# The expert stage takes its first 128 tokens ahead of the rest, and projects its routing heads in another order

## What is computed

```python
h2 = _modulate(x, norm2_g, shift2, scale2)            # RMS norm, gain, shift
qp = (h2 @ w_pq).reshape(b, s, PEER_HEADS, 2, PEER_HALF)      # 8 heads, 2 halves of 128
sc = einsum("bshpd,hpnd->bshpn", qp, sub_keys)        # 128 keys per half
s1, i1 = top_k(sc[..., 0, :], 16); s2, i2 = top_k(sc[..., 1, :], 16)
cand = s1[..., :, None] + s2[..., None, :]            # 256 candidates
top_s, top_c = top_k(cand, 16)
expert = i1[top_c // 16] * 128 + i2[top_c % 16]; gate = softmax(top_s)
# per token, 8 heads x 16 experts:
a = h2 . peer_u[expert]; w = gate * gelu(a); y = sum(w * peer_v[expert])
x = x + gate2 * y
```

## Time and profile before

| | us |
|---|---|
| median of 3 runs (3081.39 to 3085.98) | 3084.47 |
| the profiled execution, whole | 3083.38 |
| its span in the profile | 3081.6 |
| expert stage, from its first load to the end | 1707.9 to 3081.6 |

### The profile page before, as it was taken

One profiled execution on the slowest core, in us unless ns is written; L12 is line 12 of the kernel. 1 busy time (PEld: TensorE's weight loads), 2 busy tenths in 40 slices (PEclk: granted clock), 3 DMA queues, 4 the chain that ended last, 5 costly groups with the idle time before them and its releaser, 6 DMA issues. The chain is left out here.

```text
span 3081.6 us, 36160 instructions
## 1 busy us (share of the span) xinstructions
PE 2484.2 (81%) x12224; PEld 1695.7 (55%) x12224; DVE 2154.5 (70%) x3952; ACT 1006.6 (33%) x2029; POOL 1190.1 (39%) x971
## 2 busy tenths in 40 slices
PE   6998969999999798678899798766676667766665
PEld 5998969999999694244566443322222222222222
DVE  6346856777777885576334477777777878778776
ACT  2223135666666322233233222222222221222221
POOL 1444456666666430111003133443434344434442
PEclk8999989999999898787999999988889888888888
DMA  3233621221111162000301499999999999999998
GB/s 103 79 102 98 191 82 56 62 61 54 54 56 54 48 191 68 22 8 1 82 1 48 185 382 418 406 421 406 421 421 418 394 421 421 416 394 421 421 421 337
DMA packets 269756, 666.40 MB, mean 216 GB/s; under 512 B 13989, under 2 KB 201546, under 8 KB 203834
## 3 DMA queue, kind: packets, MB, share of 16 engines
q0 software_dynamic: 73728, 536.90, 42.2%
q1 hardware_dynamic: 194906, 127.75, 14.1%
q10 hardware_dynamic: 992, 0.13, 0.0%
HBM read 662.64 MB, written 2.10 MB: 216 GB/s over the span
## 5 line engine op out<-in xcount | busy, mean ns | idle before, releaser
L2106 PE MATMUL peer_py<-peer_uv,peer_diag 128*128 128x512 f32 x1536 | 841.6, 695 | 362.1 <-ACT peer_diag L2026 361.7
L1794 POOL DMA_INDIRECT peer_uv<-k_peer_uv,peer_idx x512 | 501.0, 978 | 772.6 <-PE peer_py L2106 727.9
L1906 DVE SCALAR_TENSOR_TENSOR peer_spare<-peer_uv,peer_hp 128x1024 bf16<-128x1024 f32 x512 | 622.4, 1217 | 236.5 <-DMA peer_uv<-k_peer_uv,peer_idx 236.3
L2106 PEld LDWEIGHTS peer_py<-peer_uv,peer_diag 128*128 128x128 f32 x1536 | 320.4, 221 | 844.4 <-issue 837.1
L2018 ACT ACTIVATE peer_ga<-peer_a 128x2 f32<-128x2 f32 x256 | 52.0, 203 | 843.8 <-DVE peer_spare L1906 843.8
L890 POOL TENSOR_TENSOR hgrn_wl<-p2n_w,hgrn_wh 128x1024 fp32r<-128x1024 f32 x64 | 152.5, 2393 | 231.7 <-ACT hgrn_wh L927 231.7
L1023 PE MATMUL hgrn_pp<-p2n_hh,hgrn_wh 128*128 128x264 f32 x1024 | 219.0, 295 | 17.5 <-POOL p2n_hl L340 16.7
L1023 PE MATMUL hgrn_pp<-p2n_hh,hgrn_wl 128*128 128x264 f32 x1024 | 209.6, 286 | 0.0
L1023 PE MATMUL hgrn_pp<-p2n_hl,hgrn_wh 128*128 128x264 f32 x1024 | 209.6, 286 | 0.0
L2026 ACT ACTIVATE peer_diag<-keep_ident,peer_wt 128x128 f32<-128x128 f32 x384 | 140.1, 396 | 112.1 <-DVE peer_wt L1915 111.5
L1023 PEld LDWEIGHTS hgrn_pp<-p2n_hh,hgrn_wh 128*128 128x128 f32 x1024 | 160.1, 191 | 20.7 <-issue 14.6
(11 more groups left out here) (396 smaller groups left out, 4867.2 us busy)
## 6 DMA issues: line engine op xcount, KB each, us to landing
p2n_w<-in_hgrn_w_in SPq DMA_DIRECT2D x64, 512.0 KB, 4.0
p1n_w<-in_pool_w_in SPq DMA_DIRECT2D x32, 512.0 KB, 4.0
pool_out_aw<-in_w_ada SPq DMA_DIRECT2D x16, 768.0 KB, 4.7
hgrn_out_aw<-in_w_ada SPq DMA_DIRECT2D x16, 768.0 KB, 4.9
pool_out_w<-in_pool_w_out SPq DMA_DIRECT2D x8, 1024.0 KB, 7.5
p_w<-in_w_pq SPq DMA_DIRECT2D x8, 1024.0 KB, 16.0
peer_uv<-k_peer_uv,peer_idx POOLq DMA_INDIRECT x512, 12.4
fox_wq<-in_w_in SPq DMA_DIRECT2D x12, 512.0 KB, 6.4
```

Source lines behind the costliest of these rows:

```text
L1794: pool.indirect_dma_start(out=uv[:, n % DEPTH].rearrange("p w d -> p (w d)"), out_offset=None, in_=io["k_peer_uv"], in_offset=bass.Indirec ...
L1906: dve.scalar_tensor_tensor(out=spare[:, n % 2, :], in0=uv[:, n % DEPTH, 0, :], scalar=1.0, in1=hp[:, t % 2, :], op0=ALU.mult, op1=ALU.mult ...
L2106: last = pe.matmul(py[:, h * 512:(h + 1) * 512], diag[:, products(n) % DIAGS, :], uv[:, n % DEPTH, 1, h * 512:(h + 1) * 512], start=n % (P ...
```

## The change

Three things change in `peer_phase` and the `Norm` that it uses.

1. The norm works in two spans: tokens 0 to 127 (reciprocal, eight products, eight shifts), then tokens 128 to 511. ScalarE adds the second span's shifts after it has copied the first scores.
2. Heads 0 and 1 are projected for the first 128 tokens alone, both halves in one bank with one copy (`FIRST`), and the other 384 tokens of these heads (`REST`, four pieces) later: three ahead of unit 0, the fourth in unit 0 at k = 1. Units 0 and 1 are scored right after their `FIRST` piece.
3. Head s+2 (before: s+3) is projected within unit s, for s = 0 to 5: at k = 4 and 7 in unit 0, at k = 1 and 4 in the others. ScalarE takes its halves at pairs 3 and 4 in unit 0 and at pairs 1 and 3 in the others. The scores of unit s+2 follow at k = 9 (unit 0) or k = 7, and ScalarE copies them at pair 4, that is after k = 8 and 9. VectorE routes unit s+2 in six slots, two pieces for each k from 10 to 15, for s = 0 to 5. From unit 6 on all is as before.

The weights of heads 2 and 3 are loaded when head 0, and head 1, have been projected in full. `part` is renamed `running`.

```diff
     def dve(self, dve):
         dve.wait_ge(self.rooted, 1)
-        dve.reciprocal(self.rs[:, :], self.rs[:, :]).then_inc(self.own, 1)
-        dve.wait_ge(self.own, 1)
-        for c in range(KC):
-            dve.scalar_tensor_tensor(out=self.out[:, c, :], in0=self.x[:, c, 0:self.tokens], scalar=self.gain(c),
-                                     in1=self.rs[:, :], op0=ALU.mult, op1=ALU.mult).then_inc(self.scaled, 1)
+        for i, (a, b) in enumerate(self.spans):
+            dve.reciprocal(self.rs[:, a:b], self.rs[:, a:b]).then_inc(self.own, 1)
+            dve.wait_ge(self.own, i + 1)
+            for c in range(KC):
+                dve.scalar_tensor_tensor(out=self.out[:, c, a:b], in0=self.x[:, c, a:b], scalar=self.gain(c),
+                                         in1=self.rs[:, a:b], op0=ALU.mult, op1=ALU.mult).then_inc(self.scaled, 1)
...
+        FIRST, REST, WHOLE = (0, P), (P, SEQ), (0, SEQ)
+        parts = [(0, None, FIRST), (1, None, FIRST)] + [(n, j, REST) for n in range(2) for j in range(2)] + \
+            [(n, j, WHOLE) for n in range(2, PH) for j in range(2)]
+        part_at = {e: i for i, e in enumerate(parts)}
...
             for n in range(2, PH):
-                sp.wait_ge(projected, 2 * (n - 1))
+                sp.wait_ge(projected, part_at[n - 2, 1, REST if n < 4 else WHOLE] + 1)
                 load(sp, n, n % 2)
...
-                if s == 0:
-                    return [p for p in (2 * (k - 9), 2 * (k - 9) + 1) if 0 <= p < 11]
+                if s + AHEAD < PH:
+                    return [p for p in (2 * (k - 10), 2 * (k - 10) + 1) if 0 <= p < 11]
                 return [k - 3] if 3 <= k < 14 else []
...
             norm.act(act)
-            take_q(0, 0)
-            take_q(0, 1)
+            take_q(0, None, FIRST)
             take_c(0)
+            norm.shifts(act, 1)
             act.wait_ge(x_turned, 1)
             act.activation(g2[:, :], py[:, :], ACT.Copy).then_inc(x_taken, 1)
-            take_q(1, 0)
+            take_q(1, None, FIRST)
+            take_c(1)
             take_x(0)
             exps(0)
-            take_q(1, 1)
-            take_c(1)
+            take_q(0, 0, REST)
+            take_q(0, 1, REST)
+            take_q(1, 0, REST)
             exps(1)
...
-                    if s == 0 and at in (0, 1):
-                        take_q(2, at)
-                    if s == 0 and at == 2:
-                        take_c(2)
-                    if s == 0 and at in (4, 6):
-                        take_q(3, 0 if at == 4 else 1)
-                    if s and at in (3, 5) and s + 3 < PH:
-                        take_q(s + 3, 0 if at == 3 else 1)
+                    if s == 0 and at == 1:
+                        take_q(1, 1, REST)
+                    if s + 2 < PH and at == (1 if s else 3):
+                        take_q(s + 2, 0, WHOLE)
+                    if s + 2 < PH and at == (3 if s else 4):
+                        take_q(s + 2, 1, WHOLE)
+                    if s + 2 < PH and at == 4:
+                        take_c(s + 2)
                     if at == 6 and s + AHEAD < UNITS:
                         exps(s + AHEAD)
-                if s + 3 < UNITS:
+                if PH <= s + 3 < UNITS:
                     take_c(s + 3)
...
             norm.pe(pe)
-            project(0, 0)
-            project(0, 1)
+            project(0, None, FIRST)
             scores(0)
             turn_h(0)
...
-            project(1, 0)
+            project(1, None, FIRST)
+            scores(1)
             pe.wait_ge(x_taken, 1)
             turn_x(0)
-            project(1, 1)
-            scores(1)
-            project(2, 0)
+            project(0, 0, REST)
+            project(0, 1, REST)
+            project(1, 0, REST)
...
                     if s == 0 and k == 1:
-                        project(2, 1)
-                    if s == 0 and k == 4:
-                        scores(2)
-                    if s == 0 and k in (6, 9):
-                        project(3, 0 if k == 6 else 1)
-                    if s and k in (2, 6) and s + 3 < PH:
-                        project(s + 3, 0 if k == 2 else 1)
-                    if k == (12 if s else 13) and s + 3 < UNITS:
+                        project(1, 1, REST)
+                    if s + 2 < PH and k == (1 if s else 4):
+                        project(s + 2, 0, WHOLE)
+                    if s + 2 < PH and k == (4 if s else 7):
+                        project(s + 2, 1, WHOLE)
+                    if s + 2 < PH and k == (7 if s else 9):
+                        scores(s + 2)
+                    if k == 12 and PH <= s + 3 < UNITS:
                         scores(s + 3)
```

More of the change, by code:

```diff
@@ L319, in act, with shifts @@
                        bias=self.keep["eps"][:, 0:1], scale=1.0 / D).then_inc(self.rooted, 1)
+        self.shifts(act, 0)
+    def shifts(self, act, span):
+        a, b = self.spans[span]
         for c in range(KC):
-            act.wait_ge(self.scaled, c + 1)
+            act.wait_ge(self.scaled, span * KC + c + 1)
             if self.shift is not None:
-                act.activation(self.out[:, c, :], self.out[:, c, :], ACT.Identity, bias=self.shift(c))\
+                act.activation(self.out[:, c, a:b], self.out[:, c, a:b], ACT.Identity, bias=self.shift(c))\
                    .then_inc(self.ready, 1)
@@ L1938, in store @@
                 dve.wait_ge(x_taken, t + 2)
-                dve.tensor_tensor(rows[:, t % 2, :], py[:, :], part[:, :], ALU.add).then_inc(scaled, 1)
+                dve.tensor_tensor(rows[:, t % 2, :], py[:, :], running[:, :], ALU.add).then_inc(scaled, 1)
                 dve.wait_ge(scaled, 2 * t + 1)
```

50 lines of the change are left out of this document (30 added, 20 removed).

## The result

The changed kernel takes 3090.11 us (median of 20 runs, 3087.13 to 3094.78), the kernel before 3082.46 (20 runs beside them, 3078.91 to 3086.74). The ratio is 1.0024, with a 95% interval of 1.0018 to 1.0030: 7.6 us slower. 3093 had been forecast, within 3077 to 3103.

The account below looks back on a forecast made before the run. The expert stage was taken as bound by gathers, with DMA full at 418 GB/s. Terms -2.6 + 13.0 - 3.1 = +7.3, plus 2 for the clock, gave +9.3 on 3083.4, 3092.7, called 3093 us; range 3077 to 3103.

Parts of the forecast that it names:

- First gather: Start-up up to the first gather: it was to come 13.6 us earlier (11.5 to 15), at 1731.2.
- First product: TensorE's first product, after the start-up projections: at 1750.0 instead of 1764.28, 14.3 us earlier.
- Unit 0: TensorE is the path; two k's take 3.44 us, and head 2's projection waits 2.4 us for weights landing at 1764.5.
- Scores, route, second dot of unit 1: Head 2's scores at 1786.0, VectorE's 18.2 us behind them, second dot starting at 1804.2; only 2.6 us gained.
- Units 1 to 5: Projection, scores and routing in one unit: 44.6 us each, 223.0 for five, 13.0 us more than before.
- Lead given back: In unit 6 the gathers set the pace again and a lead of 3.1 us is given back.
- Clock: TensorE's lower clock at the start of one of five units (k = 0 and 1): +2 us, ends 0 and +10.6.
- rival D: TensorE's lower clock at the start of every unit: 3102 us in all; chance 0.12.
- A: The forecast itself: units 1 to 5 paced by loop product, `take_q`, scores and route, 3086 to 3100 us; chance 0.45.
- Rival B: The eight buffers absorb the waits, units stay at 42.0 us and the early start is kept: 3073.4 us; chance 0.15.
- Rival C: Same loop but 2 us shorter in each unit (42.6 us), about even: 3084 to 3086 us; chance 0.20.
- Rival E: Weights and clock leave the first gather only 9 us earlier, costing 2 to 4 us on A: 3096 us; chance 0.08.

Follow-up runs that it names:

- experiment 3: Changed kernel with one half head projected a unit ahead: 3085.46 us; with the other half and the scores early too: 3082.62 us.
- experiment 6: Eight redundant TensorE instructions (3.43 us) ahead of the first half of heads 4 to 7: changed kernel 3101.74 us, kernel before 3092.57 us.
- Experiment 4: Changed kernel with the old unit order, head 2 projected whole ahead of unit 0, remaining tokens of heads 0 and 1 in units 5 and 6: 3069.17 us.

## Why the prediction was right, and where it wasn't

All times of after are less 4.71.

- **First gather**: forecast 1731.2, measured 1730.5. Head 0 started at 1713.5 (1714 taken), and the weights were what it waited for. The 32 instructions took 5.90 (6.2 forecast).
- **First product**: forecast 1750.0, measured 1749.2.
- **Unit 0**: forecast a wait of 2.4 us for head 2's weights. There was none to be seen: the load issued at 1744.75 was in when TensorE came to it at 1769.07, at most 24.3 us later, which fits the 23.8 of the earlier trace rows. TensorE came 2.3 us later than forecast because the first two k's ran at the lower clock (6.57 us to 1760.47, 3.44 had been taken) after 3.17 us of idleness. So head 2's projection started at 1764.4, where 1764.5 had been forecast by way of a wait that wasn't seen. That this time came out is luck: the step that failed is "two k's are 3.44". Whether a TensorE 2.3 us earlier would have met the wait no run shows.
- **Scores, route, second dot of unit 1**: forecast 1786.0 and 1804.2, measured 1785.8 and 1803.7. The 18.2 us that VectorE has behind the scores were 18.0.
- **Units 1 to 5**: forecast 44.6 each, 13.0 more than before; measured 44.3 to 44.4, 11.7 more (223.0 less 210.1 is 12.9, a slip of 0.1). Each step within the unit came as put down (25.3 to the scores, 26.3 to VectorE). ScalarE stood 6.8 us in `take_q` (8.6 in unit 0), with the gelu behind it. The experiments bear the mechanism out: the order alone makes 44.3; 3.43 us more on TensorE make 47.8; scores ready earlier take 8 us of it away.
- **Lead given back**: forecast 3.1, measured 2.2 (units 6 and 7 last 39.4 and 39.9, against 40.7 and 40.7).
- **Clock**: forecast +2 for a slow start of one unit. In units 1 to 5 the low stretch fell to k = 12 to 14 (8.11 us for 12 instructions, 5.15 at full clock), where VectorE's work was last (the next product still waits 0.21 us for its diagonal, and the second dots wait for no data), and cost nothing. The one slow start that lay on the path was that of unit 0, and it stood where the wait for weights had been put. So beside the other terms this one was too high by 2. The windows' clock, 0.88 in these units against 0.87 to 1.00 before, holds this stretch. The Trainium skill, TensorE: Matmul & The Clock Gate, Part 1, has activity release the throttle. The trace agrees: of unit 0's first instructions the eight of the product were slow (6.57 us), and those behind them ran at full speed. The rule says nothing of where in a unit the gap falls, and this decided between nothing and rival D's 3102.
- **Sum**: -3.1 + 11.7 - 2.2 = +6.5 at unit 8 (before rounding), 6.7 at the end; forecast +9.3, measured by the medians +7.6. Of the 2.9 us between 3093 and 3090.11, 2.0 are that the kernel before came out at 3082.46 in 20 runs and not at the 3084.5 that the forecast started from.
- **Chances**: two thirds of A's 0.45 are 0.30, so slower comes to 0.50, not 0.52. The forecast's own account, A, is what came.

Rival B (the buffers absorb the waits, 3073.4) is refuted: each of units 1 to 5 was over its 42.0. Its claim that "the whole loop was hidden until now" doesn't fit the kernel before either, where 13.7 us more on TensorE cost 10.6. Rival C's size (2 us less in each unit) is not what the changed kernel does; it is about what the loosened order of experiment 3 does. Rival E wasn't met.

What failed in the argument, though not in the sum, is its first step: "the expert stage is bound by the gathers: the DMA engines are full at 418 GB/s". That came from one window of 5 us. Over whole units the rate was 400, 416, 407 and 405 GB/s, and 422 only where nothing is projected. The stretch chosen lay ahead of the first projection of its unit. Taken over whole units it would have shown that the transfers alone didn't set the pace in all of them, and rival B would have deserved less than 0.15. What shared the limit, TensorE and a freed buffer by experiment 6, is read from the traces. The forecast wasn't hurt, since its 13 us were a difference from the measured 210.

Where the expected gain went, then: 14.4 us at the first gather; 11.3 of them gone by unit 1; and 11.7 more lost in five units, because a head is projected, scored and routed within one. The first loss comes about like this: in both kernels TensorE has heads 0, 1 and 2 to project in full ahead of the scores of head 2, and the changed kernel now puts eight products ahead of them too, where there were four. So these scores come 77.9 us from the stage's start, not 70.2, though the first gather is 14.4 us earlier, and VectorE's route of head 2 waits for them. Experiment 4 removes both losses and keeps the start, and this gives the 13.6 us.

## What to carry to other kernels

When work is moved out of a start-up phase, ask for each piece when it is first needed, and send the one with the latest need last. Here it was the 384 tokens of heads 0 and 1, which nobody wants until unit 8; putting them ahead of head 2 spent an early start on making head 2's scores late.

Keep what one unit makes for the next a whole unit ahead. Projection, copy, scores and routing in one unit made a loop of 44.4 us out of engines that were busy 39 and 32 us of it. And read the DMA rate over whole periods before you call a stage bound by transfers; then add work to the engine you believe is hidden, and see.

## What the runs showed of the hardware

- TensorE showed the lower of its two clock levels (1.2 GHz, of 2.4) behind pauses: 16 instructions of 512 columns took 9.71 us after 10.50 us of idleness, and 6.87 at the higher level; an instruction of 128 columns took 0.21 us at the lower level and 0.11 at the higher, in head 0's projection. Here it mattered more which instructions the slow stretch covered than how long it was: 3 us on the path at the first product of the changed kernel (8 instructions in 6.57 us), nothing at k = 12 to 14 (12 in 8.11).
- A gather issued just behind a projection, the second one after GpSimd had waited 6.9 us for a buffer, landed in 8.1 and 8.5 us in the two traces of experiment 6; the median of all is 12.4.
- The stage's first load stood between 1705.7 and 1712.6 us in the profiled executions of these kernels, behind the same code. That is as much as the effect studied, so stretches of two profiles are compared from a common event, and totals by medians.
- ScalarE's exponential began 1.29 us behind the start of its table load again (1802.56, 1803.85 in unit 0 of the changed kernel), with no pause for a drain. The Trainium skill, ScalarE: Activation LUTs, section "What ACT_TABLE_LOAD costs", gives 2.66 us for a switch with a drain of 1.38. By that figure the forecast would have been 3107, an estimate; 3090.11 was measured, and the measurement decides against it here.
